# First block's attention: the probabilities are scaled on ScalarE instead of VectorE

## The reference, cut to what matters

```python
lse = jax.nn.logsumexp(scores, axis=-1)
p = jnp.exp(scores - lse[..., None])
o = jnp.einsum('bhqk,bkhd->bqhd', p, v)   # the same for each group of windows
```

## Time and profile before

| | us |
|---|---|
| median of 3 runs | 2743.39 (2743.01 to 2744.70) |
| the profiled execution, its own time | 2743.12 |
| its span, first to last instruction | 2741.3 |
| TensorE (PE) busy in the span | 2627.9 (96%) |
| VectorE (DVE) busy | 1765.3 (64%) |
| ScalarE (ACT) busy | 1156.3 (42%) |
| GpSimd (POOL) busy | 246.8 (9%) |
| TensorE's mean granted clock | 0.987 |

### The profile page before, as it was taken

The page is one execution under the profiler, slowest core; times in us unless marked ns, Lnnn a source line. Parts: engine busy times, 40 slices in busy tenths (PEclk is TensorE's granted clock), DMA queues, the critical chain, the costliest instruction groups (busy, mean ns, idle before and its releaser), DMA issues.

```text
span 2741.3 us, 36022 instructions
## 1 busy us (share of the span) xinstructions
PE 2627.9 (96%) x14572; PEld 2102.9 (77%) x14572; DVE 1765.3 (64%) x3008; ACT 1156.3 (42%) x1906; POOL 246.8 (9%) x259
## 2 busy tenths in 40 slices
PE   4999889999999998999999999999999999999997
PEld 3877577888878676788887888777787888777776
DVE  7778658766677765878577547544536557545544
ACT  3243544333242454533234464344434464444432
POOL 0000000001200000002010031000100132000100
PEclk9999999999999999999999999999999999999999
DMA  7442024555442211455553322321322323221312
GB/s 265 139 150 92 30 78 164 173 172 167 153 129 65 65 60 52 148 177 184 195 184 106 113 66 68 97 85 51 100 72 87 102 64 95 81 87 56 100 62 77
DMA packets 256869, 302.53 MB, mean 110 GB/s; under 512 B 10176, under 2 KB 230464, under 8 KB 256704
## 3 DMA queue, kind: packets, MB, share of 16 engines
q1 hardware_dynamic: 239728, 237.10, 27.3%
q0 software_dynamic: 16688, 62.66, 7.1%
q10 hardware_dynamic: 288, 0.47, 0.1%
HBM read 289.97 MB, written 2.10 MB: 107 GB/s over the span
## 4 chain that ended last, share of the span: by engine, by line
PE 87%; DVE 9%; ACT 3%; issue 1%; DMA 0%; DVEq 0%; ACTq 0%; SPq 0%
PE ps L572 85%; PE ps L785 2%; DVE wl L1423 1%; DVE hl L1429 1%; DVE stage L1488 1%; DVE recat L1722 1%; DVE ca L1429 0%; DVE uv L1429 0%; DVE strewn L1488 0%; DVE recq L1423 0%; ACT hh L943 0%; DVE rawt L1429 0%; DVE reck L1423 0%; DVE nrm L1423 0%; ACT recat L943 0%
## 5 line engine op out<-in xcount | busy, mean ns | idle before, releaser
L572 PE MATMUL ps<-hh,wh 128*128 128x512 f32 x2208 | 887.7, 402 | 32.9 <-DVE hl L1429 17.7
L572 PE MATMUL ps<-hh,wl 128*128 128x512 f32 x2208 | 866.0, 392 | 0.0
L572 PE MATMUL ps<-hl,wh 128*128 128x512 f32 x2208 | 865.6, 392 | 0.0
L1423 DVE TENSOR_TENSOR wl<-raw,wh 128x2048 fp32r<-128x2048 f32 (+3 forms) x234 | 451.1, 1936 | 170.7 <-ACT wh L943 170.7
L572 PEld LDWEIGHTS ps<-hh,wh 128*128 128x128 f32 x2208 | 416.5, 189 | 154.6 <-issue 40.3
L572 PEld LDWEIGHTS ps<-hh,wl 128*128 128x128 f32 x2208 | 416.5, 189 | 91.2
L572 PEld LDWEIGHTS ps<-hl,wh 128*128 128x128 f32 x2208 | 417.0, 189 | 80.7
L943 ACT ACTIVATE wh<-raw 128x2048 fp32r<-128x2048 f32 (+3 forms) x234 | 370.0, 1591 | 201.4 <-PE ps L572 190.9
L572 PE MATMUL ps<-fh,wh 128*128 128x512 f32 x432 | 170.2, 394 | 0.0
L572 PE MATMUL ps<-fh,wl 128*128 128x512 f32 x432 | 168.1, 389 | 0.0
L572 PE MATMUL ps<-fl,wh 128*128 128x512 f32 x432 | 168.1, 389 | 0.0
(11 more groups left out here) (302 smaller groups left out, 3697.3 us busy)
## 6 DMA issues: line engine op xcount, KB each, us to landing
raw<-in_w_in SPq DMA_DIRECT2D x75, 1024.0 KB, 5.3
strewn<-in_w_ada POOLq DMA_DIRECT2D x104, 512.0 KB, 4.0
raw<-in_w_up SPq DMA_DIRECT2D x46, 1024.0 KB, 6.1
raw<-in_w_in SPq DMA_DIRECT2D x44, 512.0 KB, 4.9
raw<-in_w_out SPq DMA_DIRECT2D x16, 1024.0 KB, 5.2
raw<-in_w_down SPq DMA_DIRECT2D x16, 1024.0 KB, 6.8
raw<-in_w_ada SPq DMA_DIRECT2D x12, 1024.0 KB, 5.0
stage<-in_w_ada SPq DMA_DIRECT2D x8, 1024.0 KB, 11.4
```

Source lines behind the costliest of these rows:

```text
L572: return e.matmul(o, a, b, start=start, stop=stop, skip_group_check=True)
L1423: return e.tensor_tensor(o, a, b, op)
```

## The change

In the first block, VectorE takes only the reciprocal in `sn`, and the multiplication becomes a copy with a per-row scale on ScalarE, in a new function `normalize` of ScalarE's program. ScalarE waits for the reciprocal of each head by a new event `inverse`, and TensorE's wait for `probs` now goes to ScalarE's semaphore. The planner's price of a first-block `sn` becomes 0.4 us of VectorE and then 1.2 us of ScalarE. The two attentions of the second block that share the code (`cfg` "a" and "b") keep the multiplication on VectorE.

```diff
 def cost_of(unit):
+    if unit[:2] == ("sn", "1"):
+        return [("DVE", 0.4, True), ("ACT", 1.2, True)]
     if unit[0] in COST_BY_KEYS:
         n = len(keys_of(unit[1], unit[4]))
         return [(engine, us + each * n, True) for engine, us, each in COST_BY_KEYS[unit[0]]]
...
+    def normalize(cfg, l, c, i):
+        if cfg != "1":
+            return
+        rc = attention(M, cfg)[0][3]
+        for h in range(2):
+            S, x = place_of(M, cfg, c, i, h)[0], of_pair(c, i).start + h
+            go.wait_ge(*at("inverse", cfg, l, c, i, h))
+            act(S, S, ACT.Copy, scale=rc[:, x:x + 1]).then_inc(*up("act_probs", ("probs", cfg, l, c, i, h)))
+
...
-    parts = {"cb": spread, "start": start, "loaded": loaded,
+    parts = {"cb": spread, "sn": normalize, "start": start, "loaded": loaded,
...
             if cfg != "b":
                 go.wait_ge(*at("exp", cfg, l, c, i, h))
-                e.reciprocal(rc[:, x:x + 1], sm[:, x:x + 1]).then_inc(*up("dve_probs"))
+                e.reciprocal(rc[:, x:x + 1], sm[:, x:x + 1]).then_inc(*up("dve_probs", ("inverse", cfg, l, c, i, h)))
+                if cfg == "1":
+                    continue
                 go.wait_ge(*last("dve_probs"))
             ts(S[:, 0:n], S[:, 0:n], rc[:, x:x + 1], None, ALU.mult).then_inc(*up("dve_probs", ("probs", cfg, l, c, i, h)))
```

More of the change, by code:

```diff
@@ L1341, in index_scores @@
             *up("act_index", ("out", ("ts", l, i, h)), ("relu", l, i, h)))
-    parts = {"cb": spread, "start": start, "loaded": loaded, "split": split, "sq": square, "sqf": first_square, "mod": modulate, "rms": inv_rms, "row": row,
+    parts = {"cb": spread, "sn": normalize, "start": start, "loaded": loaded, "split": split, "sq": square, "sqf": first_square, "mod": modulate, "rms": inv_rms, "row": row,
              "er": early_row, "em": early_mend, "z": z, "q": q, "iv": iv, "g": g, "qk": qk, "a": a, "zs": gates, "rd": rec_diagonal, "rl": rec_level, "ra": rec_across, "ro": rec_out,
```

## The result

The median of the changed kernel is **2776.57 us** (2776.00 to 2778.24, 4 runs), that of the kernel before on the same chip 2743.87 us (2743.01 to 2744.70, 4 runs). The ratio is 1.0113, its interval 1.0086 to 1.0140: slower by 32.7 us, about six times what a measurement can tell from no change, and outside the range of 2735 to 2752 us.

A forecast was written before the change was run, and what follows sets the result against it. The prediction took TensorE, busy 96% of the span, as the bound. Saving -3.5, stage ends +4.6, table load +1.2 and blocked ScalarE +1.5 gave +3.8 us on 2743.1, so 2746.9 us, range 2735 to 2752.

The forecast's parts named there:

- VectorE's and ScalarE's work: First block's attention tiles: 48 multiplications leave VectorE, 19 us less; 48 scaled copies come to ScalarE, 29 to 34 us more.
- VectorE's saving: Both layers' mixing stages: TensorE waits less for the recurrence's products from VectorE, -3.5 us, bounds 0 and 19 us.
- The end of a stage: Last attention tiles of each layer: scaling stands behind ScalarE's result copy, 2.3 us later in the first, +4.6 us for both.
- The table load of the second layer: At 1052.26 us a pair of multiplications goes ahead of ScalarE's table load, and TensorE waits at 1056.02 us: +1.2 us.
- The blocked ScalarE at 918 us: Second layer: ScalarE's multiplications wait for late reciprocals, delaying four copies TensorE needs; 0 or 3.0 us, taken as +1.5.
- The sum: Total of the priced terms, -3.5 + 4.6 + 1.2 + 1.5 = +3.8 us, added to 2743.1 us.
- slower rival: ScalarE waits in order for VectorE's late reciprocals, at 918 and 980 us: +7.3 us, 2750.4 us; chance 30%.
- within 0.2%: Whole kernel: a change of at most 5.5 us, which a measurement can't tell from none; chance 0.43.
- faster rival: Planner places the recurrence earlier, filling idle at 260 to 281 us and the 918.53 us wait: -7.4 us, 2735.7 us; 27%.
- sign of being wrong: 260 to 281 us loses most of its 8 us idle, stages keep their length, or untouched parts change.
- place at 980 us: Second layer: reciprocals at 980.20 us, after the table load would have begun at 979.58, delay everything behind by 2.0 us.

## Why the prediction was wrong, point by point

**VectorE's and ScalarE's work: right.** 21.9 us less (forecast 19), 33.8 us more (29 to 34), 713 ns a copy (708). Two reciprocals alone hold VectorE for some 0.2 us, not the 0.38 of the text.

**VectorE's saving, −3.5 us: hardly there.** With the work moved in the old order, TensorE's waits for `reck` in layer 0 sum to 4.9 us where they were 5.2, in layer 1 to 2.2 where they were 3.3: 1.4 us.

**The end of a stage, +4.6 us: the mechanism right, the size not.** The two new waits are 1.17 and 0.97 us instead of 1.2 and 1.1. In layer 1 the stretch from the scores' wait (1056.02 before, 1075.15 us) to the last values (1066.53, 1089.71) is 14.6 us instead of 10.5. So each tail got 4.1 to 4.3 us longer, and behind it the output projection began at the low clock: from its first matmul to the feed-forward it is 76.8 us in layer 0 where it was 75.3, 1.5 us more.

**The table load of the second layer, +1.2 us: right.** The wait behind it is 3.07 us where it was 3.00, but the pair of scalings ahead of the load is paid one step earlier, by the transposes. With the work moved, then the same values before:

```profile
1067.75 1.07 PE L572 MATMUL ps<-att_p,va 128*64 128x128 f32 x16
1070.81 1.27 PE L785 MATMUL ps<-cst_r,att_s 128*128 128x128 f32 x8 [0.94 <-ACT att_s L943]
1071.39 1.28 ACT L949 ACT_TABLE_LOAD   x1
1075.15 2.08 PE L572 MATMUL ps<-ka,qa 64*128 64x512 f32 x4 [3.07 <-ACT att_p L943]
```

```profile
1049.85 1.07 PE L572 MATMUL ps<-att_p,va 128*64 128x128 f32 x16
```

From these values to the scores it is 7.40 us; before it was 6.17 (1049.85 to 1056.02), 1.2 us less.

**The blocked ScalarE at 918 us, 0 or 3.0: right where it was found.** The wait became 5.77 us, 5.7 in the text. It was 3.0, not the middle of 1.5, in the old order, and 3.7 with the matmuls around it; taking the pair apart gave the wait back.

**The sum: the step that failed** is the one that every price silently used, that TensorE's own matmuls cost the same before and after. The sum counted idle time and left TensorE's busy time at its 2627.9 us. In the changed kernel the matmuls of both layers' parts take 21.2 us more. The trace of before had the sign of it: clock 0.92 and 0.91 in the two stretches with gaps beside 1.00 in the full one, and eight transposes of 1.92 and of 1.16 us within 4 us. With the work moved in the old order, busy and idle time grew alike in sum (12.9 and 12.6 us), a microsecond of the one for each of the other, though not at each place: from 1029 to 1056 us busy time grew by 5.7 us with no new idle time. Priced so, the slower rival's 10.8 us of new waits (5.8 + 3.0 + 2.0) less 3.5 would have been 18.1 us instead of 7.3: not 27, but outside "within 0.2%".

**A second step failed: the order.** The text took the planner's freedom only as a gain ("can put the copies first", the faster rival with 27%). The order alone costs 13.0 us. The text's own sign of being wrong, that the stretch from 260 to 281 us has lost most of its 8 us of idle time, came true in the changed kernel. For that rival it was right that the recurrence moves ahead and fills the stretch 260 to 281 us; this is the changed kernel:

```profile
260.00:281.00 21.00, 18.42 (x127) 10.46 (x125) 8.67 (x19) 17.23 (x28) 0.00 (x0) 0.90 0.00 1
```

TensorE works 18.4 of 21 us where it worked 12.6, 5.9 us of idle gone, as that rival had it (7.0). What it didn't ask is where the projections that fill this stretch are then missing: behind 300 us, in a tail of 69 us instead of 48.

**The idle time** of the work in the old order, +12.6 us, is also above the +3.8 of the sum and the +7.3 of the slower rival. In layer 0 1.2 us of its 6.2 are not the move's (the wait at 207.40 us for `recq`, 5.79 instead of 4.63 us, follows a chunk of weights, for whose rounding VectorE waited 2.23 us instead of 1.09). TensorE's waits for scaled probabilities are 7.2 us in layer 0, where those for multiplied ones were 3.8, and 3.3 in layer 1 where they were 0.7; that is +6.0 us, in eight waits where there were two; the sum had looked at the last two tiles of each layer and at the pair ahead of the table load. `recat` (7.9 us instead of 4.1 in layer 1) brings 3.8. The slower rival's place at 980 us brings a wait of 1.19 us for `apad`, which stands behind the scalings and the table load; the lag grows by 1.5 us there, where the rival had 2.0. The rest isn't assigned.

The slower rival named the mechanism of the old-order part rightly, ScalarE waiting in order, and its sign came true; its price of 2750.4 was 26 us short, for the two steps above and the waits of the middle tiles; 2776.57 us lies far outside the range, whose upper end was set from that price.

## What to carry to other kernels

Here the new waits of TensorE cost about twice their length in sum, once as idle time and once in matmuls at the low clock. Where a kernel already shows a granted clock under 1.00, a sum of waits alone is therefore too low. It is no rule for the single wait: one of 3.0 us cost 3.7, and a stretch without any new idle time cost 5.0. Where a planner takes prices, a changed price is a change of its own; run it alone, and look at where the full-sized work runs out, not at how full the earlier stretch got. An engine at 42% that copies for TensorE in its program's order isn't free: 24 tiles of 1.3 us cost 27 us.

## What the runs showed that was not expected

- **Useless matmuls pay a little.** With 44 constant matmuls a layer the kernel before took 2738.36 us against 2743.62, 5.3 us less, the interval of the ratio reaching up to 0.9994; the granted clock from 1040 us to the end of the second tail rose from 0.88 to 1.00. Matmul for matmul, the two tails give 1.7 and 1.0 us. The other gains of the profiled execution, 1.5 us at 445 us and 2.7 us at about 1860 us, come from stretches at 1.2 GHz that it lacked at places where no filler stands; they are not shown to be the fillers' doing. The same fillers in another order gained nothing.
- **The fall comes after the gap, and not after every gap.** In the kernel before, TensorE has seven waits of 0.45 to 1.40 us between 1029 and 1047 us at a granted clock of 1.00 and loses it only at 1055.8 us, at the end of a wait of 3.00 us. With the work moved, the first of the seven, again 1.40 us long, has half speed behind it, from 1043.5 us on. What decides between the two isn't shown.
- **The two levels in one shape.** Eight transposes of 128x128: 1.16 us and 1.97 us; 32 products of 64x64: 2.00 and 3.68 us.
